# Seven products instead of eight in the up and gate projections of a hybrid encoder layer, with part of the weight sums made by adding DMAs

## The chip, the cores and the metric

The kernel runs on one core of a Trainium2 chip. The metric is the device time in microseconds (us). TensorE (PE) does the matrix products, VectorE (DVE), ScalarE (ACT) and GpSimd (POOL) the elementwise work, and SyncE (SP) issues most transfers.

## The reference: what is computed

One layer is applied to 544 tokens (512 of a prompt, 32 of a running stream), width 1024, all in float32:

```python
xn = rms_norm(x, g_mix);  h = xn @ w_in                     # 1024 -> 4096: u, q, k, v, two gates
merged = gate_a * (pool_branch(u) @ w_pool_up) + gate_b * (attention(q, k, v) @ w_sb_up)
x = x + merged @ w_out
x = x + square(relu(rms_norm(x, g_mlp) @ w_up)) @ w_down    # 1024 -> 4096 -> 1024
x = x + sigmoid(rms_norm(x, g_ple) @ w_ple_gate) * (p @ w_ple_proj)   # 1024 -> 1024, and 256 -> 1024
y = rms_norm(x, g_final)
```

The sum of squares of a norm is taken while x is made. The products run on x times the norm's gain, and their results are multiplied by the inverse root (`rn`) afterwards.

## The kernel before

Activations lie feature first: eight blocks of 128 features by 544 tokens, each token row cut into two halves of 272. Each float32 operand is split in two float32r parts, hi (a rounded copy, made by ACT) and lo (what is left, made by DVE), and a product is three matmuls: hi by hi, hi by lo, lo by hi.

The weights are 120 tiles of 128 by 1024, each with all of a 1024-deep contraction for 128 output columns. SP loads them into the two buffers of `raw` (L293 to L296), ACT makes `w_hi` (L403) and DVE `w_lo` (L931), in a ring of four tiles. The split of tile t + 3 is put ahead of the other work of tile t on both engines, and it waits until TensorE has finished tile t - 1. One tile makes one result (`dense`, L653 to L671): 8 blocks x 3 matmuls x 2 halves = 48 matmuls of 272 columns, with operands `a_hi`, `a_lo` or `b_hi`, `b_lo`. Results go through four slots of PSUM. A result is taken by DVE, and the next one for that slot waits for it.

In order, the stages are: the input projection with attention, the two branch projections, `w_out` (8 tiles), then four chunks of the MLP, each with 8 tiles of up and 8 of down, then 8 tiles of gate, each followed by its part of the embedding product (12 matmuls). All queues are written out by hand in program order, so an instruction waits behind everything that stands before it on its engine. In the up half DVE multiplies a result by `rn` (L968), makes square(relu) (L1199), ACT makes `b_hi` (L601) and DVE `b_lo` (L1202). In the down half DVE adds the result to x (L1177). In the w_out stage and the last down half, ACT also makes `a_hi` (L407) and the square (L413), and DVE makes `a_lo` (L936) and adds the square (L946). In the gate stage, for each of the eight tiles in turn, DVE scales (L968), ACT takes the sigmoid (L628), DVE multiplies it by the embedding product (L1227), adds it to x (L1229), ACT squares and DVE adds the square. After the last one TensorE makes the column sums (L690), DVE and ACT the inverse root, DVE the output (L1234), and SP stores it. GpSimd has nothing to do after the attention.

## Time and profile before

| | us |
|---|---|
| median of 3 runs (856.9 to 860.7) | 860.54 |
| span of the profiled execution | 858.6 |
| TensorE busy | 820.6 (96%) |
| weight loads busy | 808.8 (94%) |
| VectorE busy | 437.6 (51%) |
| ScalarE busy | 290.6 (34%) |
| GpSimd busy | 71.9 (8%) |

The span is that of one profiled execution, from its first to its last instruction, and it is the only duration that the profile gives for it. The three timed runs are other executions, and their median is 1.9 us above this span. A busy share is an average over stages; idle time on an engine that is not the one waited for costs nothing. Matmuls overlap in the records, so the distance between the starts is what one costs.

### The profile page before, as it was taken

The numbers are of one execution on the slowest core, as the hardware profiler recorded it, in microseconds if no ns is written. First come the engines' busy times: TensorE is split into PE (matmuls) and PEld (weight loads), VectorE is DVE, ScalarE is ACT, GpSimd is POOL, SyncE is SP. The second block draws the span as 40 slices with busy tenths as digits, with TensorE's granted clock in tenths as the row PEclk, the third lists the DMA queues.
The fourth block names the chain that finished last, engine by engine and source line by source line (L and its number), as shares of the span: only waits on it lengthen the run. The fifth ranks groups of instructions, "written<-read, shape, count | busy, mean of one in ns | idle before, by whom it ended". The sixth has DMA issues, their size and how long they took to land.

```text
span 858.6 us, 14955 instructions
## 1 busy us (share of the span) xinstructions
PE 820.6 (96%) x6328; PEld 808.8 (94%) x6328; DVE 437.6 (51%) x511; ACT 290.6 (34%) x337; POOL 71.9 (8%) x131
## 2 busy tenths in 40 slices
PE   4999999999996999999999999999999999999992
PEld 4999999999996989999999999999999999999992
DVE  7654454454445527655653355424553255556645
ACT  5254433424565443433221122212221122334311
POOL 6031040150240000000000000000000000000000
PEclk8999999999998989999999999999999999999996
DMA  6333131122220102521322222222222222221102
GB/s 216 106 96 123 63 113 51 67 105 74 72 79 30 70 26 74 173 86 63 108 93 95 90 82 73 98 98 73 96 89 84 98 75 79 95 97 42 59 1 104
DMA packets 22955, 73.27 MB, mean 85 GB/s; under 512 B 3329, under 2 KB 3329, under 8 KB 22913
## 3 DMA queue, kind: packets, MB, share of 16 engines
...
q0 software_dynamic: 256, 0.06, 0.0%
...
## 4 chain that ended last, share of the span: by engine, by line
PE 88%; DVE 7%; ACT 3%; issue 2%; DMA 0%; POOL 0%; DVEq 0%; SPq 0%; ACTq 0%
PE psum L662 26%; PE psum L668 26%; PE psum L665 26%; PE psum L715 3%; PE psum L643 2%; PE psum L645 2%; PE psum L644 2%; DVE a_lo L936 1%; ACT w_hi L403 1%; DVE w_lo L931 1%; DVE gates L1169 1%; DVE gates L1130 1%; DVE xt L1234 1%; PE psum L690 0%; DMA xt<-x_t 0%
## 5 line engine op out<-in xcount | busy, mean ns | idle before, releaser
L662 PE MATMUL psum<-a_hi,w_hi 128*128 128x272 f32 x1280 | 270.3, 293 | 12.3 <-DVE a_lo L936 10.9
L668 PE MATMUL psum<-a_hi,w_lo 128*128 128x272 f32 x1280 | 267.1, 290 | 0.0
L665 PE MATMUL psum<-a_lo,w_hi 128*128 128x272 f32 x1280 | 266.2, 290 | 0.0
L662 PEld LDWEIGHTS psum<-a_hi,w_hi 128*128 128x128 f32 x1280 | 202.9, 190 | 15.7 <-DVE a_lo L936 12.1
L665 PEld LDWEIGHTS psum<-a_lo,w_hi 128*128 128x128 f32 x1280 | 203.3, 190 | 0.0
L668 PEld LDWEIGHTS psum<-a_hi,w_lo 128*128 128x128 f32 x1280 | 202.2, 191 | 0.0
L931 DVE TENSOR_TENSOR w_lo<-raw,w_hi 128x1024 fp32r<-128x1024 f32 x119 | 148.3, 1246 | 75.9 <-ACT w_hi L403 74.9
L403 ACT ACTIVATE w_hi<-raw 128x1024 fp32r<-128x1024 f32 x119 | 124.9, 1050 | 131.3 <-PE psum L668 130.2
L662 PE MATMUL psum<-b_hi,w_hi 128*128 128x272 f32 x640 | 132.5, 288 | 1.2 <-DVE b_lo L1172 1.2
L668 PE MATMUL psum<-b_hi,w_lo 128*128 128x272 f32 x640 | 132.5, 288 | 0.0
L665 PE MATMUL psum<-b_lo,w_hi 128*128 128x272 f32 x640 | 131.9, 288 | 0.0
L662 PEld LDWEIGHTS psum<-b_hi,w_hi 128*128 128x128 f32 x640 | 100.6, 188 | 1.4 <-DVE b_lo L1172 1.4
L665 PEld LDWEIGHTS psum<-b_lo,w_hi 128*128 128x128 f32 x640 | 100.6, 189 | 0.0
L668 PEld LDWEIGHTS psum<-b_hi,w_lo 128*128 128x128 f32 x640 | 99.9, 189 | 0.0
L1177 DVE TENSOR_TENSOR xt<-psum,xt 128x544 f32<-128x544 f32 x40 | 29.0, 725 | 106.3 <-PE psum L668 106.3
L601 ACT ACTIVATE b_hi<-work 128x544 fp32r<-128x544 f32 x32 | 21.1, 659 | 142.2 <-DVE work L1199 142.2
L968 DVE TENSOR_TENSOR work<-psum,rn 128x544 f32<-128x544 f32 x32 | 23.2, 724 | 52.6 <-PE psum L668 52.5
L643 PE MATMUL psum<-b_hi 128*128 128x272 f32 (+4 forms) x102 | 32.6, 319 | 8.7 <-DVE gates L1021 5.5
L370 POOL TENSOR_SCALAR_AFFINE_SELECT work<-work 128x128 f32<-128x128 f32 x64 | 20.5, 354 | 211.4 <-DVE work L1000 120.7
L407 ACT ACTIVATE a_hi<-xt,vec 128x544 fp32r<-128x544 f32 x24 | 17.5, 747 | 56.8 <-DVE xt L1177 56.0
L1202 DVE TENSOR_TENSOR b_lo<-work,b_hi 128x544 fp32r<-128x544 f32 x32 | 23.2, 725 | 23.2 <-ACT b_hi L601 23.2
L645 PE MATMUL psum<-b_hi,b_lo 128*128 128x272 f32 (+4 forms) x102 | 32.2, 315 | 0.0
...
## 6 DMA issues: line engine op xcount, KB each, us to landing
raw<-w_tiles SPq DMA_DIRECT2D x119, 512.0 KB, 3.2
...
```

The costliest lines, as they stand in the source:

```text
L403: act.activation(w_hi[:, s, :, :].rearrange("p k c -> p (k c)"), raw[:, t % RAW_RING, :], ACT.Copy).then_inc(whi_done, 1)
L601: act.activation(cols(b_hi, k), work[:, (k % 2) * TOK:(k % 2 + 1) * TOK], ACT.Copy).then_inc(hhi_done, 1)
L643: pe.matmul(out, hi, rhi, start=first, stop=False, skip_group_check=True)
L645: return pe.matmul(out, lo, rhi, start=False, stop=last, skip_group_check=True)
L662: pe.matmul(base[:, h, :], w_hi[:, s, wk, :], cols(hi, k, h * HALF, (h + 1) * HALF), start=(q == 0), stop=False, skip_group_check=True)
L665: pe.matmul(base[:, h, :], w_hi[:, s, wk, :], cols(lo, k, h * HALF, (h + 1) * HALF), start=False, stop=False, skip_group_check=True)
L668: mm = pe.matmul(base[:, h, :], w_lo[:, s, wk, :], cols(hi, k, h * HALF, (h + 1) * HALF), start=False, stop=(q == len(ks) - 1), skip_group ...
L715: mm = pe.matmul(z, lhs[:, :], part[:, SOF + Z_OFF[c]:SOF + Z_OFF[c] + Z_LEN[c]], start=False, stop=(c == QB - 1), skip_group_check=True)
L931: dve.tensor_tensor(w_lo[:, s, :, :].rearrange("p k c -> p (k c)"), raw[:, t % RAW_RING, :], w_hi[:, s, :, :].rearrange("p k c -> p (k c)" ...
L968: return dve.tensor_tensor(halves(out), result(n) if banks is None else banks, halves(rn[:, :]), ALU.mult)
L1177: dve.tensor_tensor(halves(xt[:, m, :]), result(n), halves(xt[:, m, :]), ALU.add).then_inc(taken, 1)
L1202: dve.tensor_tensor(cols(b_lo, k), h, cols(b_hi, k), ALU.subtract).then_inc(hlo_done, 1)
```

## The change: what it does

The up projection of a chunk and the gate projection, each 1024 by 1024 by 544 tokens, are cut in two in each of their three dimensions, and the eight products of halves are replaced by the seven of Winograd's form of Strassen's scheme. Per quarter matrix this needs four sums of weights (`S1` to `S4`) and four of activations (`NT1`, `NT2`, `T3`, `T4`); the seven results are collected in two PSUM slots and combined into four quarters of the output. A chunk is done in two groups of 256 output columns (128 of either half), so a group has seven products of 24 matmuls and makes four 128 by 544 blocks. The gate stage has two groups as well, and four parts of the embedding product follow each.

- **Weights.** A group loads four tiles (`A11`, `A21`, `A22`, `A12`). GpSimd's queue issues a DMA that copies A21 to a buffer, a DMA that adds A22 to it (S1), and a DMA that adds A11 to A21 in place (S3). GpSimd itself adds A11 to S1 (S2) and A12 to S2 (S4). All seven are then split into hi and lo as before. `raw` gets six more buffers.
- **Activations.** `u_hi` and `u_lo` hold the seven operands. They are made once for the MLP and once for the gate, in the w_out stage and in the last down half, block by block in the order 0, 4, 1, 5, 2, 6, 3, 7, by `operand_hi` and `operand_lo`.
- **Results.** ACT copies four of the seven results out of PSUM (`copy_quarter`), DVE adds three (`add_quarter`), then DVE applies relu and `rn` to 128 by 1088 at a time (`scaled`), ACT squares that twice (`hidden_hi`), once rounded, once in place, and DVE makes `b_lo` (`hidden_lo`). In the gate stage the sigmoid, the embedding product, the residual and the square follow per group (`gate_sigmoid`, `embedded`).
- **Layout.** The MLP's chunk loop is written out. The first two tiles of a down half are done in four parts, so that they start on the blocks that are ready. New buffers lie over those of the attention. The w_out, down and other products are unchanged in size, and the embedding weights come as two more weight tiles.

```diff
+ORDER = (0, 4, 1, 5, 2, 6, 3, 7)
...
+SIDES = ("A11", "S1", "S2", "S4", "S3", "A12", "A22")
+NT1, B11, B21, B22, NT2, T3, T4 = range(7)
+OPERAND = (B11, NT1, NT2, B22, T3, B21, T4)
+IN_X = (True, False, True, False, True, False, True)
+OPENS = (True, True, False, False, False, True, False)
+BY_ACT = (True, True, True, False, False, False, True)
+LOADS = ("A11", "A21", "A22", "A12")
+UP_GROUPS = 2 * CHUNKS
+RAW_BUFS = 8
...
+def stage_results():
+    seq = [(("out", q), result_slot(N_OUT + q), False) for q in range(KT)]
+    def group(stage, g, pair, stat=None):
+        for s in range(T_UP):
+            seq.append(((stage, g, s), 2 * pair + (not IN_X[s]), BY_ACT[s]))
+            if s == 1 and stat:
+                seq.append(((stat,), 2 * (1 - pair), False))
+    for c in range(CHUNKS):
+        group("up", 2 * c, 0, "stat1" if c == 0 else None)
+        group("up", 2 * c + 1, 1)
+        seq.extend((("down", c, q), q % 4, False) for q in range(KT))
+    group("ple", 0, 0, "stat2")
+    seq.extend((("proj", q), (2 + q) % 4, False) for q in range(KT // 2))
+    group("ple", 1, 1)
+    seq.extend((("proj", KT // 2 + q), q, False) for q in range(KT // 2))
+    seq.append((("stat3",), 0, False))
+    return seq
...
+            tile = group_loads(UP_GROUPS, tile)
+            for k in range(PLE // P):
+                n = LOAD_P + k
+                sp.wait_ge(wlo_done, freed(n) + 1)
+                sp.dma_start(raw_buf(n)[:, 0:TOK], p_t[:, k, :]).then_inc(raw_in[n % RAW_BUFS], 16)
+            sp.wait_ge(wlo_done, freed(LOAD_PROJ[0]) + 1)
+            load(LOAD_PROJ[0], tile)
+            tile = group_loads(UP_GROUPS + 1, tile + 1)
+            sp.wait_ge(wlo_done, freed(LOAD_PROJ[1]) + 1)
+            load(LOAD_PROJ[1], tile)
...
+            def sums(g):
+                w = {what: raw_buf(group_load(g, what)) for what in LOADS}
+                landed = {what: (raw_in[group_load(g, what) % RAW_BUFS], raw_count(group_load(g, what)))
+                          for what in LOADS}
+                pool.wait_ge(*landed["A21"])
+                if g:
+                    pool.wait_ge(wlo_done, t_group(g - 1, SIDES.index("S1")) + 1)
+                else:
+                    pool.wait_ge(yblo_done, 2)
+                pool.dma_start(s_of[:, 0, :], w["A21"]).then_inc(s1_in, 16)
+                pool.wait_ge(*landed["A22"])
+                pool.wait_ge(*landed["A11"])
+                pool.wait_ge(s1_in, 32 * g + 16)
+                pool.dma_start(s_of[:, 0, :], w["A22"], accum_op=ALU.add).then_inc(s1_in, 16)
+                pool.dma_start(w["A21"], w["A11"], accum_op=ALU.add).then_inc(s3_in, 16)
+                pool.wait_ge(s1_in, 32 * (g + 1))
+                if g:
+                    pool.wait_ge(wlo_done, t_group(g - 1, SIDES.index("S2")) + 1)
+                    pool.wait_ge(sum_done, 2 * g)
+                pool.tensor_tensor(s_of[:, 1, :], s_of[:, 0, :], w["A11"], ALU.add).then_inc(sum_done, 1)
+                pool.wait_ge(*landed["A12"])
+                pool.wait_ge(sum_done, 2 * g + 1)
+                pool.wait_ge(s3_in, 16 * (g + 1))
+                pool.wait_ge(wlo_done, t_group(g, SIDES.index("A11")) + 1)
+                pool.tensor_tensor(w["A11"], s_of[:, 1, :], w["A12"], ALU.add).then_inc(sum_done, 1)
+            for g in range(UP_GROUPS + 2):
+                sums(g)
...
+            def operand_hi(nth, q, g):
+                m, j = ORDER[q], ORDER[q] % 4
+                first = P_B11 if m < 4 else P_B21
+                of = 8 * nth + q
+                if q >= 2:
+                    act.wait_ge(ulo_done, of - 1)
+                act.activation(parts[:, first:first + 2, :], halves(xt[:, m, :]), ACT.Copy, scale=g[:, m:m + 1])\
+                   .then_inc(xg_done, 1)
+                square(q, (nth + 1) * KT, m)
+                act.wait_ge(t_done, of + 1)
+                if m < 4:
+                    act.activation(u_hi[:, NT1:B11 + 1, j, :], parts[:, P_NT1:P_B11 + 1, :], ACT.Copy)\
+                       .then_inc(uhi_done, 1)
+                else:
+                    act.activation(u_hi[:, B21:T4 + 1, j, :], parts[:, P_B21:P_T4 + 1, :], ACT.Copy)\
+                       .then_inc(uhi_done, 1)
...
+            def copy_quarter(g, n, s):
+                act.wait_ge(full, n + 1)
+                half, token_half, sign = {"A11": (0, 0, 1.0), "S1": (1, 1, -1.0), "S2": (0, 1, 1.0),
+                                          "A22": (1, 0, -1.0)}[SIDES[s]]
+                act.activation(made(g, half, token_half), slot(n), ACT.Copy, scale=sign).then_inc(copied, 1)
+            def hidden_hi(g, half):
+                h = made_half(g, half)
+                act.wait_ge(rel_done, 2 * g + half + 1)
+                k = 4 * half + 2 * (g % 2)
+                act.activation(b_hi[:, k * TOK:(k + 2) * TOK], h, ACT.Square).then_inc(hhi_done, 1)
+                act.activation(h, h, ACT.Square).then_inc(hhi_done, 1)
+            def up_group(g):
+                for s in range(T_UP):
+                    n = NTH[("up", g, s)]
+                    ahead(t_up(g, s))
+                    if g % 2 == 1 and s == 0:
+                        hidden_hi(g - 1, 1)
+                    if g == 0 and s == 0:
+                        act.wait_ge(t_done, KT)
+                    if g == 0 and s == 1:
+                        act.wait_ge(ulo_done, KT)
+                    if g and s < 2:
+                        act.wait_ge(hlo_done, 2 * g - 1 + s)
+                    if s == T_UP - 1:
+                        hidden_hi(g, 0)
+                    if BY_ACT[s]:
+                        copy_quarter(g, n, s)
+                    if g == 0 and s == 2:
+                        act.wait_ge(taken, taken_count(NTH[("stat1",)]))
+                        root(2)
+            for c in range(CHUNKS):
+                up_group(2 * c)
+                up_group(2 * c + 1)
+                for q in range(KT):
+                    ahead(t_down(c, q))
+                    if q == 0:
+                        hidden_hi(2 * c + 1, 1)
+                    if c == CHUNKS - 1:
+                        if q == 0:
+                            act.wait_ge(hlo_done, 2 * UP_GROUPS)
+                        act.wait_ge(taken, taken_count(NTH[("down", c, q)]))
+                        operand_hi(1, q, g_ple)
...
+            def gate_sigmoid(g, half):
+                act.wait_ge(rel_done, 2 * (UP_GROUPS + g) + half + 1)
+                h = made_half(UP_GROUPS + g, half)
+                act.activation(h, h, ACT.Sigmoid).then_inc(psig_done, 1)
+            for g in range(2):
+                for s in range(T_UP):
+                    n = NTH[("ple", g, s)]
+                    ahead(t_ple(g, s))
+                    if g == 0 and s == 0:
+                        act.wait_ge(t_done, 2 * KT)
+                    if g == 0 and s == 1:
+                        act.wait_ge(ulo_done, 2 * KT)
+                    if s == T_UP - 1:
+                        gate_sigmoid(g, 0)
+                    if BY_ACT[s]:
+                        copy_quarter(UP_GROUPS + g, n, s)
+                    if g == 0 and s == 2:
+                        act.wait_ge(taken, taken_count(NTH[("stat2",)]))
+                        root(3)
+                        tables(SIGMOID)
+                        embedding_hi(0)
+                        embedding_hi(1)
+                    if g == 1 and s < 4:
+                        act.wait_ge(res_done, s + 1)
+                        square(s, 3 * KT, ORDER[s])
+                ahead(t_ple(g, T_UP))
+                gate_sigmoid(g, 1)
+                if g == 1:
                     tables(LOG_EXP)
...
+                    for q in range(KT // 2, KT):
+                        act.wait_ge(res_done, q + 1)
+                        square(q, 3 * KT, ORDER[q])
...
+                for ks, nth in (((0, 1), 1), ((4, 5), 2), ((2, 3), 3), ((6, 7), 4)):
+                    for q in range(2):
+                        t, n = t_down(c, q), NTH[("down", c, q)]
+                        if nth == 1:
+                            weights(t)
+                            place_for(n)
+                        if q == 0:
+                            pe.wait_ge(hlo_done, 4 * c + nth)
+                        mm = dense(slot(n), t % W_RING, [(k, k) for k in ks], B, opens=(nth == 1), closes=(nth == 4))
+                        if nth == 4:
+                            mm.then_inc(full, 1)
...
+            for g in range(2):
+                first = g == 0
+                group_of("ple", g, t_ple(g, 0), KT if first else None, "stat2" if first else None, 3 * KT)
+                for q in range(KT // 2):
+                    embedding(KT // 2 * g + q)
+            statistics("stat3", 4 * KT)
...
+            def operand_lo(nth, q):
+                m, j = ORDER[q], ORDER[q] % 4
+                of = 8 * nth + q
+                dve.wait_ge(xg_done, of + 1)
+                if m < 4:
+                    dve.tensor_tensor(parts[:, P_NT1, :], parts[:, P_B11, :], parts[:, P_B12, :], ALU.subtract)\
+                       .then_inc(t_done, 1)
+                    add_square(q, (nth + 1) * KT)
+                    dve.wait_ge(uhi_done, of + 1)
+                    dve.tensor_tensor(u_lo[:, NT1:B11 + 1, j, :], parts[:, P_NT1:P_B11 + 1, :],
+                                      u_hi[:, NT1:B11 + 1, j, :], ALU.subtract).then_inc(ulo_done, 1)
                 else:
...
+                    link(dve.scalar_tensor_tensor(out=parts[:, P_NT2, :], in0=parts[:, P_B22, :], scalar=-1.0,
+                                                  in1=parts[:, P_NT1, :], op0=ALU.mult, op1=ALU.subtract))
+                    link(dve.tensor_tensor(parts[:, P_T3, :], parts[:, P_B22, :], parts[:, P_B12, :], ALU.subtract))
+                    dve.scalar_tensor_tensor(out=parts[:, P_T4, :], in0=parts[:, P_NT2, :], scalar=-1.0,
+                                             in1=parts[:, P_B21, :], op0=ALU.mult, op1=ALU.subtract)\
+                       .then_inc(t_done, 1)
+                    add_square(q, (nth + 1) * KT)
+                    dve.wait_ge(uhi_done, of + 1)
+                    dve.tensor_tensor(u_lo[:, B21:T4 + 1, j, :], parts[:, P_B21:P_T4 + 1, :],
+                                      u_hi[:, B21:T4 + 1, j, :], ALU.subtract).then_inc(ulo_done, 1)
...
+            def add_quarter(g, n, s):
+                half, token_half, op = {"S4": (0, 1, ALU.add), "S3": (1, 1, ALU.subtract),
+                                        "A12": (0, 0, ALU.add)}[SIDES[s]]
+                stage = STAGED[n - N_OUT][0][0]
+                c = made(g, half, token_half)
+                dve.wait_ge(copied, copied_count(NTH[(stage, g % UP_GROUPS, 2)]))
                 dve.wait_ge(full, n + 1)
...
+                dve.tensor_tensor(c, c, slot(n), op).then_inc(taken, 1)
...
+            def scaled(g, half, relu):
+                stage = "up" if g < UP_GROUPS else "ple"
+                if half == 0:
+                    dve.wait_ge(taken, taken_count(NTH[(stage, g % UP_GROUPS, 5)]))
+                else:
+                    dve.wait_ge(copied, copied_count(NTH[(stage, g % UP_GROUPS, 6)]))
+                h = h_two if g == UP_GROUPS + 1 else h_of
+                if relu:
+                    dve.scalar_tensor_tensor(out=h[:, half, :, :], in0=h[:, half, :, :], scalar=0.0, in1=rn_twice,
+                                             op0=ALU.max, op1=ALU.mult).then_inc(rel_done, 1)
+                else:
+                    dve.tensor_tensor(h[:, half, :, :], h[:, half, :, :], rn_twice, ALU.mult).then_inc(rel_done, 1)
...
+            def up_group(g):
+                for s in range(T_UP):
+                    if s == 0 and g % 2 == 1:
+                        scaled(g - 1, 1, True)
+                    ahead(t_up(g, s))
+                    if s == 0 and g % 2 == 1:
+                        hidden_lo(g - 1, 1)
+                    if s == 2 and g == 0:
+                        statistics("stat1", 2)
+                    if not BY_ACT[s]:
+                        add_quarter(g, NTH[("up", g, s)], s)
+                    if SIDES[s] == "A12":
+                        scaled(g, 0, True)
+                    if s == T_UP - 1:
+                        hidden_lo(g, 0)
...
+            def embedded(q):
+                m, g, n = ORDER[q], q // (KT // 2), NTH[("proj", q)]
+                h = (h_two if g else h_of)[:, m // 4, m % 2, :]
+                dve.wait_ge(psig_done, 2 * g + m // 4 + 1)
+                dve.wait_ge(full, n + 1)
+                dve.tensor_tensor(halves(h), slot(n), halves(h), ALU.mult).then_inc(taken, 1)
+                dve.wait_ge(taken, taken_count(n))
+                dve.tensor_tensor(xt[:, m, :], xt[:, m, :], h, ALU.add).then_inc(res_done, 1)
+                add_square(q, 3 * KT)
+            for g in range(2):
+                for s in range(T_UP):
+                    ahead(t_ple(g, s))
+                    if s == 2 and g == 0:
+                        statistics("stat2", 3)
+                        embedding_lo(0)
+                        embedding_lo(1)
+                    if not BY_ACT[s]:
+                        add_quarter(UP_GROUPS + g, NTH[("ple", g, s)], s)
+                    if SIDES[s] == "A12":
+                        scaled(UP_GROUPS + g, 0, False)
+                scaled(UP_GROUPS + g, 1, False)
+                ahead(t_ple(g, T_UP))
+                for q in range(KT // 2):
+                    embedded(KT // 2 * g + q)
+            statistics("stat3", 4)
```

## Rows read from the trace of the kernel before

**Rows 1.** The page: span, and busy time (share) xinstructions.

```profile
span 858.6 us, 14955 instructions
PE 820.6 (96%) x6328; PEld 808.8 (94%) x6328; DVE 437.6 (51%) x511; ACT 290.6 (34%) x337; POOL 71.9 (8%) x131
```

**Rows 2.** Windows, nearly one middle chunk: us, busy (x) per engine, clock, DMA share, GB/s.

```profile
493.00:588.00 95.00, 95.00 (x760) 95.00 (x760) 42.82 (x48) 21.36 (x24) 0.00 (x0) 1.00 0.26 87
```

**Rows 3.** Timeline of DVE in a down half: start, us, operation.

```profile
471.11 0.72 DVE L1177 TENSOR_TENSOR xt<-psum,xt 128x544 f32<-128x544 f32 x1 [3.69 <-PE psum L668]
477.13 0.73 DVE L1177 TENSOR_TENSOR xt<-psum,xt 128x544 f32<-128x544 f32 x1 [3.69 <-PE psum L668]
```

**Rows 4.** Groups of instructions: busy us, mean ns of one.

```profile
L403 ACT ACTIVATE w_hi<-raw 128x1024 fp32r<-128x1024 f32 x119 | 124.9, 1050 | 131.3 <-PE psum L668 130.2 <-DMA raw<-w_tiles 0.9 <-issue 0.2
L541 ACT ACTIVATE a_hi<-psum,vec 128x544 fp32r<-128x544 f32 x4 | 2.8, 709 | 3.5 <-PE psum L645 3.5
L510 ACT ACTIVATE b_hi<-psum 128x512 fp32r<-128x512 f32 x4 | 2.3, 579 | 0.0
L476 ACT ACTIVATE b_hi<-work 128x1280 fp32r<-128x1280 f32 x8 | 10.2, 1276 | 2.6 <-POOL work L370 2.6
L1010 DVE TENSOR_TENSOR b_lo<-work,b_hi 128x1280 fp32r<-128x1280 f32 x8 | 12.2, 1527 | 5.5 <-ACT b_hi L476 5.5
```

**Rows 5.** Timeline of the first gate tile.

```profile
779.76 1.10 ACT L617 ACTIVATE b_hi<-gates 128x1088 fp32r<-128x1088 f32 x1
782.69 1.29 DVE L950 TENSOR_TENSOR b_lo<-gates,b_hi 128x1088 fp32r<-128x1088 f32 x1 [1.93 <-ACT b_hi L619]
783.61 1.08 PE L690 MATMUL psum<-work,negone 128*128 128x272 f32 x4
```

**Rows 6.** Timeline: GpSimd and DVE at once.

```profile
232.50 0.44 DVE L1078 TENSOR_TENSOR upad<-psum,rn 128x272 f32<-128x272 f32 x1
234.81 2.52 DVE L1005 TENSOR_TENSOR b_lo<-work,b_hi 128x1280 fp32r<-128x1280 f32 x1 [1.46 <-ACT b_hi L465]
234.81 1.15 POOL L350 TENSOR_TENSOR gates<-upad 128x573 f32<-128x573 f32 x1
```

**Rows 7.** DMA issues: KB each, median us to landing.

```profile
raw<-w_tiles SPq DMA_DIRECT2D x119, 512.0 KB, 3.2
pool_t<-upad POOLq DMA_DIRECT2D x8, 7.5 KB, 3.3
```

**Rows 8.** DMA while the output is stored (850 to 858 us).

```profile
GB/s 0 0 0 0 0 0 0 0 0 0 109 435 392 381 359 435 392 348 435 424 359 403 446 370 403 446 370 392 425 403 381 381 446 403 348 425 413 381 240 0
```

**Rows 9.** A gap of TensorE, and windows of 1 us in and behind it.

```profile
264.11 0.28 PE L645 MATMUL psum<-mean_hi,b_lo 128*128 128x272 f32 x1
269.94 0.59 PE L643 MATMUL psum<-b_hi 128*128 128x272 f32 x1 [5.54 <-DVE gates L1021]
266.00:267.00 1.00, 0.00 (x0) 0.00 (x0) 0.00 (x0) 0.55 (x1) 0.42 (x2) 0.92 0.36 143
273.00:274.00 1.00, 1.00 (x7) 1.00 (x6) 0.23 (x1) 0.20 (x1) 0.00 (x0) 0.66 0.00 0
```

**Rows 10.** Timeline from the start and of the end of the gate stage.

```profile
777.79 0.72 DVE L1177 TENSOR_TENSOR xt<-psum,xt 128x544 f32<-128x544 f32 x1 [1.75 <-PE psum L668]
839.00 0.29 PE L643 MATMUL psum<-b_hi 128*128 128x272 f32 x1
839.20 0.72 DVE L968 TENSOR_TENSOR gates<-psum,rn 128x544 f32<-128x544 f32 x1 [3.00 <-PE psum L668]
840.63 1.28 ACT L422 ACT_TABLE_LOAD   x1
842.99 0.72 DVE L946 TENSOR_TENSOR work<-work,ev 128x544 f32<-128x544 f32 x1 [0.72 <-ACT ev L413]
843.86 2.15 PE L690 MATMUL psum<-work,negone 128*128 128x272 f32 x4 [3.19 <-DVE work L946]
```

501 lines of the change are left out of this document (300 added, 201 removed).

## The prediction

> **What bounds the kernel now.** I read the page first: TensorE is busy 96% of the span, VectorE 51% [rows 1]. The reader should see that only TensorE can set the pace. The windows then show an MLP chunk in which TensorE never stops and runs at the full of its two clocks, 2.4 GHz [rows 2]. The timeline gives its step: one result each 6.02 us, which is 48 matmuls at 0.1252 us [rows 3]. So matmuls taken away there come off the end one for one, as long as no new wait appears. The question is whether ACT, DVE and GpSimd, with more work per matmul and in a fixed order, still keep up. I answer it by walking the queues.
>
> **What the change removes.** Per 1024 x 1024 block 14 products of 24 matmuls replace 8 of 48: 336 for 384. Five such blocks save 240 matmuls x 0.1252 = 30.1 us, of which 24.1 in the MLP and 6.0 in the gate. A product now takes L = 24 x 0.1252 = 3.01 us. The embedding product and the down half keep their matmuls.
>
> **Prices.** ACT: split 1.05, 1088 elements 1.10 (the second of two starts 1.0 later), PSUM copy 0.65 (between the 0.58 of 512 columns and the 0.71 with a scale vector), 1360 elements 1.35, from the 1.28 of 1280 [rows 4, 5]. DVE: split 1.23, 544 elements 0.72, 1088 1.29, 272 0.44, 1360 1.57, from the 1.49 of 1280 [rows 3, 4, 5, 6]. A result is seen 0.25 us after TensorE's next matmul starts [rows 10]; other hops cost 0.04. A table load takes 1.28 [rows 10].
>
> **Steady groups.** Per group ACT has 14.4 us (7 splits, 4 copies, 4 passes of 1088) and DVE 15.9 (7 splits, 3 adds, 4 passes) in 7L = 21.0, so neither is the bound; order may be. Let T be the end of an even group's seventh product. DVE: add of A12 from T-2.75, `scaled` from -2.0 to -0.7. ACT: two squares -0.7 to 1.4 (`hidden_hi` stands ahead of `copy_quarter`), copy to 2.0, split to 2.9. DVE: `hidden_lo` to 2.8, `scaled` of the other half to 4.0. ACT: its squares to 6.1, and only then the copy of the odd group's first product, to 6.7. The third product goes into that slot and wants to start at T+6.0: 0.7 us lost, four times, 2.8. With the copy at 0.58 or 0.71 it is 0.6 to 0.8. After an odd group the down half follows, where the same chain ends at T+7.5 and is wanted at T+9.0, thanks to the four parts: nothing lost. Other places have more room: a split is made three products (9 us) ahead of its use, and a slot is wanted again one product (3 us) after its result.
>
> **Operands.** Per w_out tile DVE now needs 1.23 + 0.72, then 1.9 or 3.6: 9.4 us per two tiles of 12.0. The last block's chain (residual 0.72, ACT scale 0.7, three sums 1.4, `u_hi` 1.35, `u_lo` 1.57, and the hops) ends 6.1 us behind the stage. It is wanted by the third product, at 6.0 + 1.0 for the statistics [rows 5]: hidden by 0.9. In the last down half the four parts make it 0.5 late. In the MLP's first group DVE waits for the root before it can add S4, and the sixth product starts 0.5 late.
>
> **Adding DMAs.** No row shows one. From below: a plain 512 KB load lands in 3.2 us [rows 7]. For a copy I take 3.3, which a GpSimd-issued transfer of 7.5 KB takes [rows 7], plus 512 KB at 400 GB/s, 1.3 [rows 8]: 4.6. An adding one reads twice: 3.3 + 2.6 = 5.9, my value. From above: nothing in the rows forbids that adding elements is several times slower, so I ask from where it matters. S1 of an odd group may start when S1 of the even one is split, 9.5 us before the down half ends; it is wanted 15.2 us after that end. Copy and add fit up to an add of 20 us. Even groups have more. Tight are two places. In group 0 A21 can only be loaded late in w_out (landing 18.5 us before its end), so S1 is there 8.0 us before that end, just as DVE needs its turn for the seventh residual: hidden. In the gate's second group A21 waits for a buffer freed by S4's split: landed 11.2 us into the stage, S1 at 21.7, wanted at 21.8. Each is hidden at 5.9, and costs up to 1 us per us beyond an add of about 8 and 9.
>
> The Trainium skill (Collectives: The Full Stack, The bandwidth ceiling: the fold count and why AG ≠ RS ≠ AR) holds that adding in the DMA engines halves the rate because of the second read, and is not slow by itself; with DMA: Bandwidth & Descriptors (Anatomy of one DMA — SWDGE (gpsimd) path), 2.0 us plus bytes at 436 GB/s, that would be 4.4 us. The trace before has no adding DMA.
>
> **GpSimd's sums.** 1024 elements at 1.15/573 [rows 6]: 2.1 us, two per group. With both engines at it, a DVE operation of 1.49 took 2.52, longer by about GpSimd's 1.15 [rows 6]. In the MLP these sums fall where DVE has slack. In group 0 they fall on the last two operand blocks (0.8 us), in the gate's first group on `scaled` and two splits: up to 4 us on DVE, of which 1.7 is slack; I take 0.7.
>
> The Trainium skill (SBUF — State Buffer, Who interferes with whom) has a rule that speaks against the change: a VectorE operation with two SBUF inputs and a GpSimd operation that reads SBUF exclude each other for the whole instruction. The pair above agrees.
>
> **The gate stage, from its start U.** Before, from U = 777.75 to the last column sums at 843.86: 66.1 us [rows 10]. After, in us behind U: the third product runs 7.0 to 10.0, and ACT makes the root only behind its copy of that result (to 12.3), so DVE has `rn` at 14.6. On ACT the table load and the two embedding blocks then stand before the split for the seventh product (to 15.9); on DVE the two embedding blocks and that split stand before the add of the fourth product (S4), which ends at 17.9. The sixth product wanted its slot at 16.1: 1.9 lost. Seventh ends at 24.0, embedding parts at 30.0. DVE's `embedded(0)` to `(3)` stand before its splits for the second group, and each ends with a square that ACT makes only behind its copy of product (1, q). So (1,1) waits for the slot that `embedded(1)` empties at 35.7: 2.7 lost. `embedded(2)` is done at 43.9, `embedded(3)` at 46.9, the split for (1,3) at 48.1; TensorE wanted it at 41.75: 6.4 lost. In a gap of 5.5 us the granted clock fell to 1.2 GHz, and it came back 3.5 us after work resumed [rows 9]: 1.8 more. The group ends at 61.9. Behind it come the copy (62.9), `scaled` (64.3), the sigmoid (65.5) and the table load (66.8), and then four times in turn multiply, add, ACT's square, add, 2.9 us each: the last square is added at 76.9. Before, seven of those eight rounds lay under TensorE's work. The stage takes 76.95, or 10.85 longer. With 0.5 and 0.7 from above, 12.05.
>
> **Sum.** -24.05 + 2.8 + 0.5 + 0.8 + 12.05 = -7.9: span 858.6 to 850.7. The median stands 1.9 above the span of that execution, so 860.5 - 7.9 = 852.6. A difference under 0.5% (4.3 us) can't be told from none.
>
> **Rivals.** *All hidden:* the saved matmuls count in full, 860.5 - 30.1 = 830.4; for it speaks only the DVE's idle half [rows 1], against it the order above. If only the gate stalls are half of what I have, 846. Chance 0.15 for below 846. *Slow adds:* one mechanism, the time of an adding DMA. At 12 us group 0 loses 4.3 and the gate 3.2, the gain is gone; from there each us costs two. From 14.5 it is slower by 0.5%, at 20 us it is 876. For it: an untested operation, fp32 words added one by one; against: the fast plain transfers [rows 7, 8]. Chance 0.16 for slower than 864.8. *GpSimd's lock lands on the path:* all 20 sums x 2.1 would be 41 us, but only those near the odd group's second and third product and in the gate count. If each of five groups lost one, 10.5, it would be 863, in the range of no change; with milder slow adds 0.22 for 856.2 to 864.8. *The change doesn't shorten the product:* if 272-column matmuls in the new order took over 0.143 us, 7/8 would save nothing; nothing in the rows makes the order matter, so under 0.03, inside the last two. My forecast, 846 to 856.2, has 0.47.
>
> So faster 0.62, same 0.22, slower 0.16. The range 840 to 866 takes in the slow add up to 15 us and part of the better case.
>
> **What would show it.** Right: starts of TensorE 3.0 us per product; about 0.7 us idle before the third product of four odd groups, released by ACT's copy; three gaps in the gate stage near 2, 2.7 and 6.4 us, the last released by DVE's split behind `embedded(3)`; the clock at 0.5 behind it; the last column sums 77 us into the stage. Adding DMAs landing in 4 to 8 us. Wrong: splits by ACT that wait for the adding DMA in the MLP, a DVE split at 2 to 3 us beside GpSimd in a steady group, or a gate stage under 70 us.

## The result: slower by 1.5%, against a forecast of 0.9% faster

The changed kernel takes 873.1 us (870.8 to 873.9, 4 runs), the kernel before beside it 858.7 us (856.9 to 860.7, 4 runs): ratio 1.0152, 95% interval 1.0115 to 1.0189. The forecast was 852.6 us, with 840 to 866 as its range.

The page of the changed kernel, to set beside [rows 1]:

```profile
span 869.0 us, 14316 instructions
PE 798.5 (92%) x6088; PEld 785.2 (90%) x6088; DVE 502.4 (58%) x537; ACT 372.7 (43%) x421; POOL 146.4 (17%) x181
```

The 240 matmuls are gone (6328 to 6088), yet TensorE is busy only 22.1 us less, and it idles more. I cut both traces at the same four marks: the end of w_out, the first matmul of the gate stage, the last column sums, the end.

| stretch | before | after | difference | forecast |
|---|---|---|---|---|
| start to end of w_out | 391.82 | 388.85 | -3.0 | 0 |
| the MLP | 385.78 | 381.13 | -4.7 | -20.0 |
| gate stage to last column sums | 66.26 | 84.27 | +18.0 | +12.05 |
| rest | 14.7 | 14.75 | 0 | 0 |
| span | 858.6 | 869.0 | +10.4 | -7.9 |

The first matmul of the gate stage before starts at 777.60, where the forecast had 777.75. The first stretch is nearly all code that the change leaves as it is; TensorE's granted clock rose earlier in this execution (0.94 between 16 and 20 us, 0.50 before). It is not a gain to count on: in the runs below w_out ends between 388.8 and 392.1 us.

Next the timeline of TensorE, those rows that begin behind an idle time of over 0.5 us (the number in brackets, with its releaser), and the last column sums.

```profile
399.77 0.57 PE L1197 MATMUL psum<-u_hi,w_hi 128*128 128x272 f32 x1 [10.92 <-DVE w_lo L1289]
...
432.87 0.36 PE L1197 MATMUL psum<-u_hi,w_hi 128*128 128x272 f32 x1 [1.77 <-ACT h_of L859]
...
524.14 0.36 PE L1197 MATMUL psum<-u_hi,w_hi 128*128 128x272 f32 x1 [0.55 <-ACT h_of L859]
...
773.94 0.39 PE L1197 MATMUL psum<-u_hi,w_hi 128*128 128x272 f32 x1 [2.67 <-DVE u_lo L1539]
...
792.22 0.36 PE L1197 MATMUL psum<-u_hi,w_hi 128*128 128x272 f32 x1 [1.59 <-DVE w_lo L1289]
...
806.58 0.36 PE L1197 MATMUL psum<-u_hi,w_hi 128*128 128x272 f32 x1 [2.02 <-DVE h_of L1632]
...
812.30 0.56 PE L1197 MATMUL psum<-u_hi,w_hi 128*128 128x272 f32 x1 [2.46 <-DVE h_of L1632]
...
825.89 0.59 PE L1197 MATMUL psum<-u_hi,w_hi 128*128 128x272 f32 x1 [5.99 <-DVE w_lo L1289]
...
854.25 2.15 PE L1208 MATMUL psum<-work,negone 128*128 128x272 f32 x4 [8.61 <-DVE work L1305]
```

The row at 524.14 comes twice more, 91.27 us apart. The reader should see one gap of 10.92 us ahead of the MLP's first product, which the forecast didn't have, and then a gate stage with the forecast's three gaps (1.59, 2.46, 5.99 for 1.9, 2.7, 6.4) and two more, of 2.67 and 2.02 us. Windows behind the first gap and behind the one at the gate's start show the half clock (columns as in [rows 2]):

```profile
400.00:405.00 5.00, 5.00 (x23) 5.00 (x24) 3.67 (x6) 3.30 (x4) 2.12 (x3) 0.50 0.91 173
774.00:777.50 3.50, 3.50 (x17) 3.50 (x18) 2.56 (x4) 1.35 (x3) 0.00 (x0) 0.54 0.00 0
```

What stood before the 10.92 us gap, from the timelines of SP and GpSimd (idle time before, and its releaser, in brackets), then ACT and DVE:

```profile
372.11 0.34 SPq L455 DMA_DIRECT2D raw<-w_tiles  x1
372.49 2.87 SPq L455 DMA_DIRECT2D raw_more<-w_tiles  x6
376.00 0.60 POOL L601 DMA_DIRECT2D s_of<-raw  x1 [71.20 <-DMA raw<-w_tiles]
385.50 0.90 POOL L605 DMA_DIRECT2D s_of<-raw_more  x1 [8.89 <-DMA s_of<-raw]
386.07 1.25 POOL L606 DMA_DIRECT2D raw<-raw  x1
390.20 2.35 POOL L611 TENSOR_TENSOR s_of<-s_of,raw 128x1024 f32<-128x1024 f32 x1 [2.89 <-DMA s_of<-raw_more]
392.88 2.96 POOL L616 TENSOR_TENSOR raw<-s_of,raw_more 128x1024 f32<-128x1024 f32 x1 [0.33 <-DMA raw<-raw]
```

```profile
390.15 1.06 ACT L642 ACTIVATE w_hi<-s_of 128x1024 fp32r<-128x1024 f32 x1 [8.97 <-DMA s_of<-raw_more]
```

```profile
369.37 1.58 DVE L1550 TENSOR_TENSOR u_lo<-h_of,u_hi 128x1360 fp32r<-128x1360 f32 x1 [0.77 <-ACT u_hi L844]
370.86 1.22 DVE L1289 TENSOR_TENSOR w_lo<-raw,w_hi 128x1024 fp32r<-128x1024 f32 x1
...
391.24 2.39 DVE L1289 TENSOR_TENSOR w_lo<-s_of,w_hi 128x1024 fp32r<-128x1024 f32 x1 [8.45 <-ACT w_hi L642]
393.56 0.71 DVE L1527 TENSOR_TENSOR xt<-psum,xt 128x544 f32<-128x544 f32 x1
395.08 1.06 DVE L1535 TENSOR_TENSOR h_of<-h_of 128x272 f32<-128x272 f32 x1 [0.82 <-ACT h_of L836]
...
397.81 1.23 DVE L1289 TENSOR_TENSOR w_lo<-s_of,w_hi 128x1024 fp32r<-128x1024 f32 x1 [0.22 <-ACT w_hi L642]
398.96 0.72 DVE L1527 TENSOR_TENSOR xt<-psum,xt 128x544 f32<-128x544 f32 x1
```

Read from the end. The first product starts at 399.77, as the residual of w_out's last result empties its slot at 399.68 (the view names the split ahead of it). That residual stands on DVE behind the splits of S2 and S1. S1's split waited for the adding DMA, issued at 385.50 and landed at 390.1: 4.6 us, so it is not slow. It was issued late because the plain copy of A21 ahead of it, issued at 376.00, took 8.9 us to land. Six other loads had been issued just before it. (Times of DMAs are from issue to landing; GpSimd's next issue starts 0.6 us after the landing that it waited for.)

### The profile page after: what moved, and what is told of

The parts are those of the page before. It is cut to its first block, busy times and chain, and to the rows that moved or that the text cites. A ratio compares the mean times of both kernels' runs of the same rounds, so it can differ in the third digit from the quotient of the medians.

```text
span 869.0 us, 14316 instructions
## 1 busy us (share of the span) xinstructions
PE 798.5 (92%) x6088; PEld 785.2 (90%) x6088; DVE 502.4 (58%) x537; ACT 372.7 (43%) x421; POOL 146.4 (17%) x181
## 4 chain that ended last, share of the span: by engine, by line
PE 66%; DVE 17%; ACT 9%; issue 4%; DMA 2%; POOL 0%; DVEq 0%; SPq 0%; ACTq 0%; POOLq 0%
PE psum L1197 19%; PE psum L969 14%; PE psum L975 13%; PE psum L972 13%; DVE w_lo L1289 4%; PE psum L1022 2%; PE psum L950 1%; ACT w_hi L634 1%; PE psum L952 1%; PE psum L951 1%; ACT h_of L836 1%; ACT w_hi L642 1%; DVE u_lo L1550 1%; DMA s_of<-raw 1%; DVE xt L1527 1%
## 5 line engine op out<-in xcount | busy, mean ns | idle before, releaser
L1197 PE MATMUL psum<-u_hi,w_hi 128*128 128x272 f32 x560 | 166.3, 297 | 29.2 <-DVE w_lo L1289 18.5
L1197 PE MATMUL psum<-u_lo,w_hi 128*128 128x272 f32 x560 | 164.8, 294 | 0.0
L1197 PE MATMUL psum<-u_hi,w_lo 128*128 128x272 f32 x560 | 164.7, 294 | 0.0
L969 PE MATMUL psum<-a_hi,w_hi 128*128 128x272 f32 x640 | 137.2, 296 | 11.5 <-DVE a_lo L1295 10.3
L1197 PEld LDWEIGHTS psum<-u_hi,w_hi 128*128 128x128 f32 x560 | 108.8, 194 | 31.4 <-DVE w_lo L1289 21.3
L975 PE MATMUL psum<-a_hi,w_lo 128*128 128x272 f32 x640 | 133.8, 291 | 0.0
L972 PE MATMUL psum<-a_lo,w_hi 128*128 128x272 f32 x640 | 133.4, 290 | 0.0
L1197 PEld LDWEIGHTS psum<-u_lo,w_hi 128*128 128x128 f32 x560 | 108.6, 194 | 0.1
L1197 PEld LDWEIGHTS psum<-u_hi,w_lo 128*128 128x128 f32 x560 | 108.4, 194 | 0.0
L972 PEld LDWEIGHTS psum<-a_lo,w_hi 128*128 128x128 f32 x640 | 102.1, 191 | 0.0
```

The source lines that it names most:

```text
L969: pe.matmul(base[:, h, :], w_hi[:, s, wk, :], cols(hi, k, h * HALF, (h + 1) * HALF), start=(opens and q == 0), stop=False, skip_group_chec ...
L972: pe.matmul(base[:, h, :], w_hi[:, s, wk, :], cols(lo, k, h * HALF, (h + 1) * HALF), start=False, stop=False, skip_group_check=True)
L975: mm = pe.matmul(base[:, h, :], w_lo[:, s, wk, :], cols(hi, k, h * HALF, (h + 1) * HALF), start=False, stop=(closes and q == len(ks) - 1), ...
L1197: mm = pe.matmul(out[:, two, :], w_part[:, t % W_RING, 2 * k + two, :], u_part[:, op, k, :], start=(OPENS[s] and k == 0 and w_part is w_hi ...
```

## The experiments

Each kernel ran beside the kernel before on the same chip; the latter's median lay between 858.7 and 859.5 us in all five series. Unless its text names another, an edit starts from the changed kernel.

### Group 0: why is S1 late, and is it only late?

**e1_loads_first**: SP issues the loads into the six new buffers as soon as those are free, 361 us into the run, and A11 and A21 behind them.

```diff
-for what in LOADS of group 0, 1, ...: in order of the tiles
+for n in range(RAW_RING, RAW_BUFS): load(n, T_MLP + n)      # six buffers
+for n in range(RAW_RING): wait_ge(wlo_done, ...); load(n, T_MLP + n)
```

> Six of the first eight loads of the MLP are issued ahead of A11 and A21 of group 0, which still wait for their two buffers. The theory (the 10.9 us gap ahead of the MLP has two causes: A21 lands only 13.1 us before the w_out stage ends, and the copy behind it takes 8.9 us because the six loads, 3 MB, run beside it) expects the copy at 4 to 5 us, S1 4 to 5 us earlier, the gap at 6 to 7 us, and a time 4 to 5 us under that of the changed kernel, so about 1.01 of before. A rival (the adding DMA or GpSimd's issue is slow in itself there) expects a gap as before, 10 to 11 us, and the same time. A second rival (A21's landing alone decides, with a copy whose time doesn't change) expects the same too.

Measured 866.6 us, ratio 1.0100 (1.0056 to 1.0144). GpSimd's and TensorE's timelines:

```profile
375.79 0.60 POOL L609 DMA_DIRECT2D s_of<-raw  x1 [71.18 <-DMA raw<-w_tiles]
379.28 0.90 POOL L613 DMA_DIRECT2D s_of<-raw_more  x1 [2.90 <-DMA s_of<-raw]
```

```profile
393.65 0.57 PE L1205 MATMUL psum<-u_hi,w_hi 128*128 128x272 f32 x1 [4.82 <-DVE w_lo L1297]
```

The copy is issued at the same time as in the changed kernel (375.79 for 376.00) and lands after 2.9 us instead of 8.9. S1 landed at 383.9 and the gap fell from 10.9 to 4.8 us. So the crowd of loads made the copy slow.

**e2_a21_early**: e1, and group 0 loads A21 and A22 into the first new buffers; the first add of every group no longer waits for A11.

```diff
+ORDERS = {0: ("A11", "A12", "A21", "A22")}    # the last two: buffers that are free early
```

> As the first, and in group 0 A21 and A22 change places with A11 and A12, so that they land in free buffers before the w_out stage is at its fifth tile; the first add of each group no longer waits for A11. If S1 of group 0 is all that holds the MLP's start, the gap of 10.9 us and the 2.6 us at the lower clock behind it go, and the gap of 1.8 us in the second group falls to about 0.6: 13 to 15 us under the changed kernel, level with before (ratio 0.998 to 1.003). If the rival is right that ACT and DVE can't make the operands in the w_out stage in time anyway (as in the last down half, 2.7 us late), a gap of 2 to 4 us stays and the gain is 8 to 11 us.

Measured 868.0 us, 1.0111 (1.0077 to 1.0144). S1 landed at 380.9, 3.0 us sooner than in e1, and the gap stayed: 5.0 us. So S1's landing no longer sets it, and both expectations on the time fail. The copy, now beside the six loads, took 8.7 us again.

**e5_a21_quiet**: e2, and group 1's four loads stand behind A11's and A12's on SP.

```diff
-for n in range(RAW_RING, RAW_BUFS): load(n)        # then 0 and 1
+for n in range(RAW_RING, 4): load(n)               # then 0 and 1, then 4 to 7
```

> As the kernel with A21 and A22 of group 0 loaded first (868.0 us, a gap of 5.0 us before the MLP), but group 1's four loads are issued behind A11 and A12, so the copy of A21 runs beside few loads. Theory (copy crowded, then GpSimd's lock, then a slot): copy takes 3.5 to 4.5 us instead of 9.2, S1 has landed about 5 us earlier, at 14 to 16 us before w_out's end. GpSimd's two sums come earlier, one of them no longer on the last block's operand chain. What remains of the gap is at least 1.1 us, because the first product's slot is that of w_out's last result, which DVE can empty only 0.25 + 0.72 us behind it; with one sum still beside DVE's last operands 1.1 to 3.5 us. Time 864 to 867 us. Rival (the gap is S1's landing alone): gap 0 to 0.3 us, 863. Rival (crowding was not the cause): copy still near 9 us, gap near 5, 868.

Measured 867.4 us, 1.0084 (1.0057 to 1.0112). The copy took 5.8 us, and the add, now beside A12, group 1's four loads and the S3 add, 9.8 (374.80 to 384.6). The crowd had moved on to the add. Gap 4.3 us. The expectation missed that.

**e10_held**: e5, and group 1's loads wait until S1 has landed.

```diff
+sp.wait_ge(s1_in, 32)
 for n in range(4, RAW_BUFS): load(n, T_MLP + n)
```

> As the kernel in which group 1's loads stand behind A11 and A12 (867.4 us, gap 4.34, copy 6.3 us and add 9.8 us), but group 1's loads are held until S1 of group 0 has landed; group 0's own four loads stay beside the copy. Theory (copy, adds and loads share one total of about 0.4 MB per us, so each lasts as long as the bytes queued with it): beside the add now run only A12's load and the S3 add, about 2.5 MB moved, 5 to 7 us instead of 9.8; S1 has landed by 379 to 382, 7 us or more before w_out's end, and what is left is the slot's wait (at least 1.1 us) and GpSimd's sums: gap 1.1 to 3 us, 862 to 866 us. Rival (an adding DMA beside the S3 add is slow by itself): add still over 9 us, gap over 4.

Measured 868.0 us, 1.0102 (1.0064 to 1.0139). The add took 7.1 us and S1 landed at 382.1, 10.0 us before w_out's end (392.12); but the gap is 4.98 us, outside what I expected. GpSimd's timeline and DVE's show why:

```profile
382.14 2.38 POOL L629 TENSOR_TENSOR s_of<-s_of,raw 128x1024 f32<-128x1024 f32 x1 [5.36 <-DMA s_of<-raw_more]
384.76 2.40 POOL L634 TENSOR_TENSOR raw<-s_of,raw 128x1024 f32<-128x1024 f32 x1 [0.23 <-DMA raw_more<-raw]
```

```profile
382.15 2.67 DVE L1562 TENSOR_TENSOR h_of<-h_of 128x272 f32<-128x272 f32 x1
384.86 2.60 DVE L1563 SCALAR_TENSOR_TENSOR h_of<-h_of 128x272 f32<-128x272 f32 x1
```

These two sums take 0.44 us each elsewhere. They wait out GpSimd's two, 4.4 us in all, in the middle of the operand chain. The Trainium skill (SBUF — State Buffer, Who interferes with whom) says that a VectorE operation with two SBUF inputs and a GpSimd operation that reads SBUF exclude each other for the whole instruction; the pairs above agree.

**e14_held_dma0**: e10, with the loads held until S2 has landed, and S2 and S4 of group 0 are made by a copy and three adding DMAs.

```diff
-pool.tensor_tensor(s_of[:, 1, :], s_of[:, 0, :], w["A11"], ALU.add)      # S2, g == 0
-pool.tensor_tensor(w["A11"], s_of[:, 1, :], w["A12"], ALU.add)           # S4
+pool.dma_start(s_of[:, 1, :], w["A11"])
+pool.dma_start(s_of[:, 1, :], s_of[:, 0, :], accum_op=ALU.add)           # S2
+pool.dma_start(w["A11"], w["A12"], accum_op=ALU.add)
+pool.dma_start(w["A11"], s_of[:, 0, :], accum_op=ALU.add)                # S4
```

> As the kernel with group 1's loads held (868.0 us, gap of 4.98 us before the MLP, in which two sums of 128x272 on DVE took 2.67 and 2.60 us beside GpSimd's two), but S2 and S4 of group 0 alone are made by a copy and adding DMAs, and group 1's loads are held until S2 has landed. Slots as in the changed kernel. Theory (with S1 early, GpSimd's sums of group 0 are the whole rest but for the slot): the two operations on DVE take 0.44 us each, and the gap falls to 1.0 to 1.5 us, which is the wait for w_out's last result; 862.5 to 865 us. Rival (the operand chain is late by itself): gap still 4 us or more, 867 to 869. Rival (S2's adding DMA lands late): DVE and ACT idle for a DMA, gap of 1 us, then one of 2 to 5 us before the third product, 866 to 869.

Measured 871.3 us, 1.0138 (1.0118 to 1.0157). ACT's and TensorE's timelines:

```profile
390.85 1.06 ACT L684 ACTIVATE w_hi<-s_of 128x1024 fp32r<-128x1024 f32 x1 [1.48 <-DMA s_of<-s_of]
...
403.01 1.06 ACT L684 ACTIVATE w_hi<-raw 128x1024 fp32r<-128x1024 f32 x1 [5.62 <-DMA raw<-s_of]
403.98 0.61 ACT L901 ACTIVATE h_of<-psum 128x544 f32<-128x544 f32 x1
```

```profile
393.90 0.36 PE L1239 MATMUL psum<-u_hi,w_hi 128*128 128x272 f32 x1 [2.20 <-DVE w_lo L1331]
...
404.68 0.56 PE L1239 MATMUL psum<-u_hi,w_hi 128*128 128x272 f32 x1 [3.57 <-issue]
...
418.74 0.36 PE L1239 MATMUL psum<-u_hi,w_hi 128*128 128x272 f32 x1 [2.23 <-DVE w_lo L1331]
```

All of DVE's sums there are back at 0.44 us and the gap is 2.2 instead of 4.98: with S1 early, GpSimd's sums were the cause of 2.8 us at least. In what is left S2's DMA has its share: ACT waits 1.5 us for it, and w_out's last residual stands behind that split. But S4, two adding DMAs in turn, is now late: ACT waits 5.6 us for it, and only then copies the first product out of the slot that the third one needs (the row at 403.98). So the gap of 3.6 stands before the third product, where the rival with the late DMA had it, but the DMA is S4's and not S2's. The theory holds for DVE's sums and fails on the time.

**e12_slots**: only the result slots change, so that the first product doesn't share one with w_out's last result.

```diff
-return seq
+return [(name, at if name[0] == "out" else (at + 2) % 4, by) for name, at, by in seq]
```

> The changed kernel with nothing but the result slots exchanged in pairs from the MLP on, so that the first product doesn't need the slot of w_out's last result. Theory: the first product starts at w_out's end on the blocks that are there and stops for its last block, whose residual stands behind the late split of S1; most of the 10.9 us gap stays, 2 to 4 us go: 869 to 871 us. Rival (the slot is the whole wait): the gap before the first product goes to under 1 us with none behind it, 861. Rival (the slot is no wait at all): same as the changed kernel, 873.

Measured 871.7 us, 1.0129 (1.0097 to 1.0161). The first product starts at w_out's end, runs on three of its four blocks and stops for 7.79 us, released by `u_lo` of the block whose residual stands behind S1's split. So the slot is a part of the wait, and the operands are next in line. Of the 3.1 us that the gap lost, 1.4 come back as a new gap at 419.85, ahead of the group's sixth product: DVE makes the root before it can add the fourth result. The time is 1.4 us under the changed kernel's, and the two intervals overlap.

### GpSimd's sums elsewhere

**e4_short_sums**: S2 and S4 are made on 64 of 1024 columns only, in all groups but the first (the rest of these sums is left out).

```diff
+wide = slice(0, 64 if g else D_MODEL)
-pool.tensor_tensor(s_of[:, 1, :], s_of[:, 0, :], w["A11"], ALU.add)
+pool.tensor_tensor(s_of[:, 1, wide], s_of[:, 0, wide], w["A11"][:, wide], ALU.add)
```

> GpSimd's own two sums are 64 columns wide instead of 1024 in all groups but the first, so S2 and S4 are left unmade there; loads, adding DMAs and all waits are as in the changed kernel. The theory (the exclusive use of SBUF by GpSimd's sums lengthens single VectorE operations by 1.0 to 2.2 us where VectorE is on the path: last down half, gate stage) expects no VectorE split over 1.4 us behind group 0, the gap at the gate's start 1 to 2.5 us shorter, the scaling of 3.1 and the split of 3.4 us at 1.3 and 1.2, the gate stage 3 to 6 us shorter, the MLP's chunks the same. The rival (GpSimd's sums fall beside VectorE's slack everywhere) expects under 1 us.

Measured 866.4 us, 1.0090 (1.0067 to 1.0113), 0.6% under the changed kernel. The gaps of 1.77, 2.67 and 2.02 us become 0.56, 0.21 and none; 2.46 and 5.99 stay. So 1.2, 2.5 and 2.0 us of these three are the lock's. For the last one, the changed kernel's timelines of DVE and GpSimd:

```profile
796.34 3.13 DVE L1580 TENSOR_TENSOR h_of<-h_of,rn 128x1088 f32<-128x1088 f32 x1
802.38 3.42 DVE L1289 TENSOR_TENSOR w_lo<-s_of,w_hi 128x1024 fp32r<-128x1024 f32 x1
```

```profile
795.93 2.40 POOL L611 TENSOR_TENSOR s_of<-s_of,raw_more 128x1024 f32<-128x1024 f32 x1 [3.90 <-DMA s_of<-raw]
801.34 3.38 POOL L616 TENSOR_TENSOR raw_more<-s_of,raw_more 128x1024 f32<-128x1024 f32 x1 [3.02 <-DMA raw<-raw_more]
```

In e4 the two operations of DVE take 1.29 and 1.22 us.

**e6_dma_sums**: S2 and S4 by DMAs, as in e14, in all groups.

> The changed kernel with S2 and S4 made by copies and adding DMAs too, so that GpSimd computes nothing from the MLP on. Same sums, four more DMAs per group. Theory (GpSimd's lock on DVE costs 3.5 to 4 us by the run with short sums): the 1.77 us gap of the first odd group becomes 0.55, the 2.67 us gap at the start of the gate stage under 0.7, with its cold clock; group 0's gap stays near 11 us. If the DMAs land as before (4.6 us each, two in turn behind S1), time 865 to 868 us. Rival (the adding DMAs share bandwidth and slow each other and the loads): S2 or S4 late in group 0 and in the gate's second group, where S1 lands with nothing to spare; waits of ACT for DMA there of 2 to 5 us each, time 869 to 876.

Measured 885.1 us, 1.0292 (1.0271 to 1.0313), worse than the rival had it. DMA issues (count, size, median us to landing), and ACT in the first odd group:

```profile
s_of<-s_of POOLq DMA_DIRECT2D x10, 512.0 KB, 7.9
raw_more<-raw_more POOLq DMA_DIRECT2D x9, 512.0 KB, 8.1
```

```profile
428.73 1.06 ACT L647 ACTIVATE w_hi<-s_of 128x1024 fp32r<-128x1024 f32 x1 [6.88 <-DMA s_of<-s_of]
...
436.00 1.06 ACT L647 ACTIVATE w_hi<-raw_more 128x1024 fp32r<-128x1024 f32 x1 [3.70 <-DMA raw_more<-s_of]
```

Here ACT waits for DMAs in the middle of the MLP, and the gap there is 6.56 us for 1.77. At the gate's start, where the sums have time, the gap is 0.18 for 2.67. (e4 also made S2 and S4 ready earlier; here they come later and the gap goes all the same, so it is the lock's.) Here the DMA is the better adder where time is left, and GpSimd where it isn't.

### Order on ACT and DVE

**e3_gate_squares**: in the gate's second group ACT makes each square of the first four blocks at the head of a step, ahead of its split and its copy, instead of at the step's end; DVE adds it behind its split (`ahead`) instead of in `embedded`. In the last four blocks each sum stands one block later.

```diff
 ahead(t_ple(g, s))
+if g == 1 and s < 4: add_square(s, 3 * KT)      # DVE; was the end of embedded(q)
```

> Only the gate stage's order is changed: the squares of x and their adds are taken out of the round of embedded(q); ACT makes a square at the head of a step of the second group and DVE adds it behind its split, and at the end multiply and add of the next block stand ahead of the add of the last square. The theory (DVE's splits and a PSUM slot wait behind ACT's squares, which wait behind its copies) expects the gaps of 2.5 and 6.0 us in the second group and most of the 3.3 us at the lower clock to go, and the tail to be 2 to 3 us shorter: 12 to 15 us under the changed kernel. The rival (the adding DMAs and GpSimd's sums set this stage's pace) expects the same gaps with another releaser and under 4 us of gain.

Measured 857.7 us, ratio 0.9990 (0.9976 to 1.0004), 15.4 us less than the changed kernel. The gaps of 2.46 and 5.99 are gone, and the idle time before the last column sums is 4.98 us for 8.61. The gate's stage runs from 770.18 to the last column sums at 839.30, 69.1 us for 84.3.

**e7_copy_first**: e3, and in odd groups `hidden_hi(g - 1, 1)` stands behind `copy_quarter` of the first product.

> The kernel with the gate stage's squares moved (857.7 us) and in odd groups ACT's copy of the first product put ahead of the squares of the even group's second half. Theory: the three gaps of 0.55 us and most of the 1.77 us one, all released by ACT, go: 1.7 to 2.9 us less, 855 to 856.2 us, and nothing new appears, since the two squares are wanted only by the down half. Rival (the moved squares delay ACT's next split): a new gap of some 0.5 us one product later, 857.5 us.

Measured 852.4 us, 0.9922 (0.9892 to 0.9952). The gaps of 1.78 and three times 0.56 become 0.22 and none. By the spans (854.1 to 851.4) the edit gives 2.7 us, as expected; the medians lie 5.3 apart, and these two kernels were not measured side by side.

### All together

**e8_all**: e7 with e5's loads, e6's sums, e12's slots, and A21 and A22 first in the gate's second group too.

> All edits at once: A21 and A22 of group 0 and of the gate's second group first, group 1's loads later, all weight sums by DMAs, ACT's copy first in odd groups, the gate's squares moved, and all result slots from the MLP on exchanged in pairs, so that the first product doesn't wait for w_out's last result. Theory: of the changed kernel's 873 us go 11 to 13 us before the MLP with its cold clock, 3 of ACT's order, 4 of the lock, 15 of the gate stage: 838 to 843 us, gap before the MLP under 1.5 us, three chunks of 90.6 us. Rival (edits don't add up: another queue, above all ACT's or DVE's own work in group 0, takes over): gaps of 3 to 6 us stay before the MLP and in the gate stage, 846 to 852 us.

Measured 851.2 us, 0.9899 (0.988 to 0.9919): the rival's time, but only in part its places. Gaps of 1.66 and 1.86 us stand behind the MLP's second product and one of 4.44 us in the first odd group, where ACT waits 6.7 and 3.7 us for DMA sums; in the gate stage none is over 1.82 us until the last column sums.

**e9_held_all**: e8 with GpSimd's sums as in the changed kernel and e10's held loads.

> All edits except the sums by DMAs: GpSimd makes S2 and S4 as in the changed kernel; A21 and A22 first in group 0 and in the gate's second group; group 1's loads held until S1 of group 0 has landed; result slots exchanged in pairs; ACT's copy first in odd groups; the gate's squares moved. Theory: from the run with the squares moved and the copy first (852.4 us) go the 11.0 us gap before the MLP and the 2 to 3 us of cold clock behind it, and 0 to 2.5 us of gap come back for GpSimd's sums on the last operands: 838 to 843 us. Rival (the DMAs can't be made quick enough, whatever is held): gap of 4 us or more, 845 to 848.

Measured 844.1 us, 0.9818 (0.9794 to 0.9842), a little over the theory. The gap ahead of the MLP is spread over 1.13, 0.99, 0.56 and 1.44 us, and 2.65 us are left at the gate's start.

**e11_mixed**: e9 with DMA sums in the gate's first group alone.

> The first kernel of this call, with S2 and S4 of the gate's first group alone made by adding DMAs, whose sums stood beside DVE's operands for the gate in the last down half. Theory (lock): the gap of 2.7 us at the gate's start goes below 0.5, 1 to 4 us less than the first kernel with the clock's share. Rival (four more DMAs delay the gate's second group or ACT's splits): no difference, or up to 3 us more.

Measured 840.4 us, 0.9781 (0.9757 to 0.9804), the fastest; span 838.4. Four of its gaps, by TensorE's timeline:

```profile
392.46 0.39 PE L1234 MATMUL psum<-u_hi,w_hi 128*128 128x272 f32 x1 [1.52 <-DVE u_lo L1576]
...
411.19 0.36 PE L1234 MATMUL psum<-u_hi,w_hi 128*128 128x272 f32 x1 [1.43 <-DVE w_lo L1326]
...
759.95 0.39 PE L1234 MATMUL psum<-u_hi,w_hi 128*128 128x272 f32 x1 [0.19 <-DVE u_lo L1576]
...
778.24 0.36 PE L1234 MATMUL psum<-u_hi,w_hi 128*128 128x272 f32 x1 [1.81 <-DVE w_lo L1326]
```

The gap at the gate's start is 0.19. From w_out's end (389.65) to the gate's first matmul (758.48) are 368.8 us, 17.0 less than before, and the gate stage takes 65.2, 1.1 less, with 4.97 us idle before the last column sums for 3.19 before the change. So of the 24.1 us that the matmuls promise in the MLP the scheme gives 17.0, and of the 6.0 in the gate 1.1, once the orders on SP, ACT and DVE and the slots are changed and one group's sums go to the DMA.

**e13_mixed_two**: e11 with DMA sums in group 0 too.

> The mixed kernel (840.4 us) with group 0's S2 and S4 made by adding DMAs too. Theory: the gaps of 1.5, 0.6 and 1.4 us in and behind the first products of the MLP go, 1 to 3 us less: 837.5 to 839.5 us. Rival (S2 of group 0 lands late, as three DMAs share the total with A12's load): a gap of 2 to 4 us before the third product, 841 to 843.

Measured 845.7 us, 0.9843 (0.9825 to 0.9861). A gap of 5.0 us stands behind the MLP's second product, where ACT waited 5.9 us for S4: the rival's gap in its place, with S4 for S2, and larger. In group 0 GpSimd's sums cost less than the DMAs.

## Why the prediction was wrong, point by point

- **The step that failed** is the one on group 0: A21 "landing 18.5 us before its end", copy 4.6 and add 5.9, "so S1 is there 8.0 us before that end ... hidden". S1 landed 1.3 us behind it. A21 landed at 375.7, 13.1 us before the end, because the split that frees its buffer (370.86) stood on DVE behind an operand chain (5.4 us later than I had it); the copy took 8.9 us instead of 4.6 (4.3); GpSimd issued each DMA 0.3 and 0.6 us behind the landing that it waited for (0.9). The add was 4.6, 1.3 better than my value. That makes 5.4 + 4.3 + 0.9 - 1.3 = 9.3, from 8.0 before the end to 1.3 behind it. I had the time of each DMA as if it ran alone, and hadn't listed what SP issues beside it, though the six new buffers were free and their loads follow A21's in one go. The gap of 10.9 and the half clock behind it, 2.7 us (5.9 us in which matmuls start 0.227 us apart for 0.125), make 13.6 for the 1.3 in the sum.
- **What took its place.** With S1 early, 4.3 to 5.0 us stay. At least 2.8 of them are GpSimd's lock (e14), for which I had 0.8 in group 0: e10 shows two lengthened operations, back to back and each as long as GpSimd's sum, on a chain with no slack left. And I had missed that the first product shares its slot with w_out's last result, which alone is about 1 us, by an estimate from the 0.25 and 0.72 us of the rows.
- **The matmuls saved** hold: 240 fewer. The chunks repeat in 91.27 us; less the gap of 0.55 a product takes 3.02 us of it (a thirtieth), and a chunk is 0.58 more than 720 matmuls at 0.1252, or 2.3 us in four chunks. The account of the MLP: -24.05 + 13.6 + 3.4 (1.77 and three of 0.55) + 2.3 = -4.75, measured -4.7.
- **The sixth product** of the MLP's first group, 0.5 late in the sum, isn't late in the changed kernel, and 1.4 us late in e9, e11 and e12, where the first product starts at w_out's end.
- **ACT's order in odd groups**, "0.7 us lost, four times", was right in place and releaser: 0.55 three times, and 1.77 in the first, where a split of 3.10 us on DVE (420.35) comes on top. In the steady groups splits of 2.7 to 3.0 us stand beside GpSimd's sums at four more places (460 to 643 us), one of my signs of being wrong, but no gap of TensorE follows: they fall where DVE has slack, as I had it.
- **The gate stage**, +12.05, measured +18.0. Its three gaps stood within 0.4 us of the forecast, the tail is 14.8 us from the seventh product's end for 15.0, and moving the squares took the last two gaps out (e3). Mis-sized was again the lock: 2.67 us at the start for 0.5, a gap of 2.02 that I didn't have, and two more stretches of half clock, 1.6 and 1.4 us, less the 0.7 that I had put in for it and 1.0 by which the forecast's own terms were too large: 2.2 + 2.0 + 1.6 + 1.4 - 0.7 - 1.0 = 5.5 of the 5.95 missing. I had put it at up to 4 us on DVE, of which 1.7 is slack. The two rows in e4 are 1.8 and 2.2 us longer than without GpSimd's sums, 4.0 in all, and 4.0 less 1.7 is near the gap of 2.02; the wrong step was to take 0.7.
- **The rival of slow adds** is false: the adds for S1 land in 4.5 to 5.9 us. Those for S3, issued right behind them, take 6.6 to 10.3, more than the 4 to 8 that I had as a sign of being right. An estimate by the Trainium skill (DMA: Bandwidth & Descriptors, Anatomy of one DMA — SWDGE (gpsimd) path) was 4.4, and the trace agrees for S1's add in group 0, with 4.6. **The lock's rival** was real but not alone: e4 takes 0.6% off. **The chances** had 0.16 on slower, all of it on the add's speed. The mechanism that ended slower, a crowd on the DMA engines ahead of the add, was not among the rivals.
